# Two passes over 256 tokens in place of one over 512, in the gate and up products of four feed-forwards

## What is computed

```python
D_FF = ((8 * D_MODEL // 3 + 127) // 128) * 128      # 2816 = 22 * 128

def swiglu_2(h, w_gu, w_down):
    gu = h @ w_gu
    g, u = jnp.split(gu, 2, axis=-1)
    return (jax.nn.silu(g) * u) @ w_down

# twice (once for each layer):
h = modulate(x, g_norm[l, 0], mod[:, 0], mod[:, 1])
x = x + 0.5 * mod[:, 2][:, None, :] * swiglu_2(h, w_ffn1_gu[l], w_ffn1_down[l])
x = x + mod[:, 5][:, None, :] * hybrid_mixer(...)
h = modulate(x, g_norm[l, 2], mod[:, 6], mod[:, 7])
x = x + 0.5 * mod[:, 8][:, None, :] * swiglu_2(h, w_ffn2_gu[l], w_ffn2_down[l])
```

## Time and profile before

| | us |
|---|---|
| median of 2 runs (3003.88 and 3004.03) | 3003.95 |
| span of the profiled execution | 2999.2 |
| median less the span | 4.75 |
| PE busy (13,800 matmuls) | 2885.2 |
| PEld busy (13,800 weight loads) | 2294.2 |
| DVE busy | 1808.9 |
| ACT busy | 1307.9 |

### The profile page before, as it was taken

How to read it: one execution, slowest core, us unless ns; L and a number is a source line. 1 busy time by engine, 2 the same in 40 slices (tenths; PEclk the granted TensorE clock), 3 DMA queues, 4 the chain that set the end, 5 groups by cost and what they waited for, 6 DMA issues and landing times. The chain is left out here.

```text
span 2999.2 us, 39355 instructions
## 1 busy us (share of the span) xinstructions
PE 2885.2 (96%) x13800; PEld 2294.2 (76%) x13800; DVE 1808.9 (60%) x2177; ACT 1307.9 (44%) x1512; POOL 326.0 (11%) x425
## 2 busy tenths in 40 slices
PE   8999798999999999999999999999999999999998
PEld 4876566777777778888877788887888877788886
DVE  7747857999999987555158555425554156533323
ACT  5125535888888863233136322213322136332312
POOL 0100012333333320000000000000000000000000
PEclk9989999999999999999999999999999999999999
DMA  8552236999999996553222255423554222122221
GB/s 320 169 197 92 100 152 247 370 361 372 373 365 355 367 367 237 192 188 134 98 102 71 94 200 195 154 95 106 193 194 154 98 96 77 65 104 98 97 87 68
DMA packets 115843, 555.50 MB, mean 185 GB/s; under 512 B 20656, under 2 KB 22192, under 8 KB 73776
## 3 DMA queue, kind: packets, MB, share of 16 engines
q1 hardware_dynamic: 89264, 491.43, 44.3%
q0 software_dynamic: 26496, 62.96, 5.9%
HBM read 549.10 MB, written 37.75 MB: 196 GB/s over the span
## 5 line engine op out<-in xcount | busy, mean ns | idle before, releaser
L168 ACT ACTIVATE stream_high<-stream_raw 128x2048 fp32r<-128x2048 f32 x151 | 289.3, 1917 | 799.8 <-PE ffn_ps_psum L470 755.0
L173 DVE TENSOR_TENSOR stream_low<-stream_raw,stream_high 128x2048 fp32r<-128x2048 f32 x156 | 356.7, 2287 | 406.9 <-ACT stream_high L168 406.5
L468 PE MATMUL ffn_ps_psum<-h_high_f,stream_high 128*128 128x512 f32 x1344 | 523.3, 389 | 0.2 <-DVE stream_low L173 0.2
L470 PE MATMUL ffn_ps_psum<-h_high_f,stream_low 128*128 128x512 f32 x1344 | 522.8, 389 | 0.0
L469 PE MATMUL ffn_ps_psum<-h_low_f,stream_high 128*128 128x512 f32 x1344 | 522.8, 389 | 0.0
L312 DVE TENSOR_TENSOR expert_low<-expert_raw,expert_high 128x2048 fp32r<-128x2048 f32 x128 | 292.8, 2288 | 6.1 <-ACT expert_high L308 2.5
L692 DVE TENSOR_TENSOR ffn_sg<-ffn_sg,ffn_ps_psum 128x512 f32<-128x512 f32 x88 | 60.5, 687 | 388.5 <-PE ffn_ps_psum L470 385.6
L468 PEld LDWEIGHTS ffn_ps_psum<-h_high_f,stream_high 128*128 128x128 f32 x1344 | 252.3, 188 | 53.5 <-DVE stream_low L173 0.6
L469 PEld LDWEIGHTS ffn_ps_psum<-h_low_f,stream_high 128*128 128x128 f32 x1344 | 252.3, 188 | 52.8 <-issue 0.2
L470 PEld LDWEIGHTS ffn_ps_psum<-h_high_f,stream_low 128*128 128x128 f32 x1344 | 252.3, 188 | 51.8
L468 PE MATMUL ffn_ps_psum<-ffn_hid_high,stream_high 128*128 (+1 forms) x704 | 277.6, 394 | 3.2 <-DVE ffn_sg L692 3.2
(11 more groups left out here) (497 smaller groups left out, 5050.7 us busy)
## 6 DMA issues: line engine op xcount, KB each, us to landing
expert_raw<-in_exp_gu SPq DMA_DIRECT2D x128, 1024.0 KB
stream_raw<-in_ffn_gu SPq DMA_DIRECT2D x88, 1024.0 KB, 5.0
expert_raw<-in_exp_dn SPq DMA_DIRECT2D x64, 1024.0 KB
con<-in_w_mod SPq DMA_DIRECT2D x120, 512.0 KB
stream_raw<-in_ffn_dn SPq DMA_DIRECT2D x44, 1024.0 KB, 5.0
mix_mod_rows<-in_w_ada POOLq DMA_DIRECT2D x32, 512.0 KB
stream_raw<-in_w_in SPq DMA_DIRECT2D x16, 1024.0 KB, 5.0
pieces_raw<-in_w_in SPq DMA_DIRECT2D x11, 1024.0 KB, 6.9
```

The costliest lines, as they stand in the source:

```text
L168: self.nc.scalar.activation(self.high[:, q], self.raw[:, q], ACT.Copy).then_inc(self.high_done, 1)
L173: self.nc.vector.tensor_tensor(self.low[:, q], self.raw[:, q], self.high[:, q].bitcast(F32), ALU.subtract)\
L468: mm(out, w[0], x[0], start=start, stop=False)
L470: return mm(out, w[1], x[0], start=False, stop=stop)
```

## The change

Each of the three matmuls of a slice is made as two, over tokens 0 to 255 and 256 to 511, both with the same weights, into the two halves of the same bank. The `start` flag stands only on the first matmul of the bank, the `stop` flag only on the last. The semaphore increments stay on the last matmul of each bank.

```diff
+HALF_S = S // 2
...
                     def up_piece(s, bank, k):
                         c = slice((2 * k + bank) * P, (2 * k + bank + 1) * P)
-                        return self.mm3(ps[:, 2 * s + bank, :], w.part(s, c), (h[0][:, k, :], h[1][:, k, :]),
-                                        start=k == 0, stop=k == KD - 1)
+                        high, low = w.part(s, c)
+                        for weight, x in ((high, h[0]), (high, h[1]), (low, h[0])):
+                            for n in range(2):
+                                mm = nc.tensor.matmul(ps[:, 2 * s + bank, n * HALF_S:(n + 1) * HALF_S], weight,
+                                                      x[:, k, n * HALF_S:(n + 1) * HALF_S],
+                                                      start=k == 0 and x is h[0] and weight is high and n == 0,
+                                                      stop=k == KD - 1 and weight is low and n == 1)
+                        return mm
```

## The result

| | us |
|---|---|
| before, median of 2 runs | 3003.95 |
| after, median of 2 runs (3057.35 and 3064.43) | 3060.89 |
| ratio, with its 95% interval | 1.0193 (1.0161 to 1.0225) |
| span of the profiled execution after | 3062.3 |

The changed kernel is slower by 1.9%. Five more runs of it, beside nine of the kernel before on another chip, gave 3062.85 against 3011.15 us, a ratio of 1.0178 (1.0157 to 1.0198).

The account below looks back on a forecast made before the run. The prediction took the matmul stream's rate on PE as the bound. 4032 x (230.0 - 226.7) = +13.3 us on 3003.95 us gave 3017.3 us, with a range of 2990 to 3100 us.

Parts of the forecast that it names:

- What bounds the kernel: In the feed-forwards' up blocks only the matmul stream's rate sets the time; 4032 matmuls at 226.7 ns, 914 us.
- The counts and what hides: In the up blocks 4032 matmuls become 8064, with 4032 added weight loads; DVE, ACT and softer edges cost nothing.
- The weight load's rate: In the up blocks a load is hidden if the matmul beside it lasts 112 ns; fp32 rows gave 111.8 ns.
- Rival (D): Weight loads in the up blocks don't overlap: 188 ns for each matmul, 3606 us; chance 0.04.
- The loop's code: The up loop's body grows from 192 to 384 loads and matmuls; bound 20 us, nothing taken.
- Rival (C): The longer up loop doesn't stay on the chip, every round waits for code: up to +117 us, 3121 us; chance 0.07.
- The 13.3 ns: Each up matmul's time beyond its columns, taken as partly a rate: t = 115.0 ns for 256 columns, +13.3 us.
- rival (A): The extra is paid once for each up matmul: 120.0 ns for 256 columns, +53.6 us, 3057.6 us; chance 0.28.
- 0.43: Chance of the forecast's own case for the up matmuls, 2991 to 3030 us.
- 0.28: Chance that each up matmul pays the extra once, 3057.6 us.

Follow-up runs that it names:

- Experiments 3: Changed kernel with only the gate products split, the up products back in one pass of 512 tokens: 3033.58 us, ratio 1.0090 to the kernel before.
- 10: Changed kernel with the down products split in two halves of tokens as well: 3083.99 us, ratio 1.0251 to the kernel before.
- 4: Changed kernel with four passes of 128 tokens instead of two of 256: 3890.03 us in one run, kernel before 3011.15.
- 5: Changed kernel with each pass cut in 384 and 128 tokens instead of 256 and 256: 3247.68 us in one run, kernel before 3007.44.
- experiment 2: Changed kernel with all three products of one token half first, then those of the other: 3060.52 us, ratio 1.0167 to the kernel before.
- Experiment 6: Changed kernel with each slice multiplied for one half of the tokens only, 4032 matmuls of 256 columns: 2661.16 us in one run.
- experiment 9: Changed kernel, six of eight slices using 32 of 128 weight columns, 256 tokens in gate and 128 in up: 3035.99 us, kernel before 3007.22.
- experiments 7: Gate and up products with bf16 operands, in whole passes of 512 columns like the kernel before: 2974.90 us in one run, kernel before 3007.44.
- 8: Gate and up products with bf16 operands, in two passes of 256 columns like the changed kernel: 2976.56 us in one run, kernel before 3007.44.
- 12: Kernel before with feed-forward corrections in bf16, activations densely copied, products grouped by type, no split: 2979.09 us, ratio 0.9894 to the kernel before.

## Why the prediction came out as it did

**What bounds the kernel: right.** The stretches stayed full on PE at clock 1.00, and every nanosecond of spacing arrived in the time: 4032 x 13.3 ns = 53.6 us by the sum, and the same by the four stretches. Experiments 3 and 10 follow that sum with other counts, and 4 and 5 with the load's 111.7 ns where a matmul is shorter than its neighbour's load.

**The counts and what hides: right.** There are 8064 matmuls and as many loads; equal weights are loaded twice and don't matter (experiment 2); DVE, ACT and the softer edges cost nothing. Experiment 6 shows where that cover ends: when a block falls from about 10.9 to 5.8 us, DVE's splitting is late.

**The weight load's rate: right, as a floor.** 111.8 ns came from fp32 rows and was measured at 111.7 in fp32r (experiment 4). Rival (D), 188 ns, is out: the load's 192 ns are a latency and hide behind matmuls 120 ns apart. The page "TensorE: Matmul & The Clock Gate" of the Trainium skill, section "What overlaps and what doesn't", says that a load overlaps a running matmul only when it goes to other rows of the array; 8064 full 128 by 128 loads at 120.0 ns disagree with it.

**The loop's code: right to take nothing.** Rival (C) is out by the two instruction queues above and by experiment 4, whose body is four times that of before.

**The 13.3 ns: here the prediction failed.** The step is "I take the first, because a stretch that lies inside the duration looks like a rate": a 5 ns stretch for half the columns, t = 115.0. Measured were 120.0, with the duration at 283 ns against my 277. The term was 13.3 us and should have been 53.6, so the likeliest point lies 44 us below the measured median, and rival (A)'s 3057.6 us lies 3.3 below it. The range held because (A) was in it, and not by the forecast's own sum. That the kernels differ by less than 2% held narrowly: the ratio of 1.0178 lies below with its whole interval, that of 1.0193 reaches over it with the upper end of its own. That the part lies inside the duration told nothing of how it grows with columns; one 512-column size can't tell a rate from a start, and the trace had only that size in this type. So the choice between 0.43 and 0.28 rested on a likeness alone.

**The other half of that step was misleading too.** "It isn't the weight load", I wrote, since matmuls with 24-column weights are also 230 ns apart. For 256 columns the load does matter: 120.0 ns with 128 columns of weights, 113.3 with 32 (experiment 9). So rival (A) had the right time and not the right mechanism; a price of 13.3 ns whatever is loaded is refuted. It doesn't look like a rate either: with 32-column loads the extra is 6.7 ns for 256 tokens and 6.7 for 128.

**What stays open** is why fp32r pays this. Start to start less columns / 2.4, by size of tokens and weights: 512 and 128, 13.3 ns; 256 and 128, 13.3; 256 and 32, 6.7; 128 and 32, 6.7; 512 and 24, about 17 in the stretch of the earlier trace rows, where DVE was busy for 97% of the time. Two readings are left, both only argued.

The first: the moving operand comes in a little slower than the array takes it (6.7 ns for 256 columns, 13.3 for 512), a full load costs 13.3 ns of its own, and the larger of the two shows. It fits the first three values. The fourth should be 3.3; the short load's own rate could be what shows there, but the rows of 223 ns are shorter than those of 276 by just the 53 ns of 128 columns, so they show no wait for a load.

The second: the extra goes with the weight columns of the load and not with the tokens, 13.3 ns beside 128 and 6.7 beside 32. It fits the first four. Against it, none of the 14 spacings of the 24-column matmuls from 172.2 to 175.4 us is under 224 ns, 10.7 above the columns. And in fp32 a full load of 4-byte weights costs nothing like it, as the kernel before shows:

```profile
1107.81 4.45 PE L2737 MATMUL experts_x_psum<-hT,shared_wg 128*128 128x512 f32 x10
```

Ten starts, with a row of 592 ns for the last, are (4.45 - 0.59) / 9 = 429 ns each. At two steps a column 512 columns take 426.7 ns, so the extra is some 2.5 ns. So neither 4-byte operands nor their full loads bring the 13.3 ns by themselves. The size that would settle it, 512 tokens with 32 weight columns in a feed-forward stretch, wasn't run. What is shown: the extra belongs to fp32r operands (10.8 ns of it are gone in experiments 7 and 8), it is smaller with a short load (experiment 9), and with full loads each additional matmul of 256 columns costs 13.3 ns (the changed kernel, experiments 2, 3, 6 and 10).

**The 9.5 us ahead of the feed-forwards** are no part of any step; the change doesn't reach there, and runs of one kernel differ by as much.

## What to carry to other kernels

Read a dense stream's rate from its starts, take away columns / clock, and ask of the remainder how it depends on each operand; if the trace has only one size, the two readings are even until another size is measured. In fp32r with a full load for each matmul, two matmuls of 256 columns cost 13.3 ns more than one of 512, and below the load's own 112 ns fewer columns save nothing; in bf16 the split costs 2.5 ns. Of a product in three parts, the corrections can go in bf16; here that paid when they were densely laid and grouped by type, and not with neither (the two weren't tried apart).

## What the runs showed of the hardware

- fp32r, full 128 by 128 loads, start to start: 226.7 ns for 512 columns, 120.0 for 256, 111.7 for 128. With 32-column loads 113.3 for 256 and 60.0 for 128.
- bf16, full loads (98 ns long): 215.8 ns for 512 columns, 109.2 for 256. The 256-column bf16 stream ran below the 111.7 ns that is the floor of full fp32r loads, so with bf16 weights the floor is lower.
- A 384-column and a 128-column fp32r matmul in turn took 286.6 ns: the wide one's load, which starts beside the narrow matmul, isn't hidden.
- fp32, full loads, 512 columns: 429 ns, some 2.5 above two steps a column.
- bf16 read with a step of two as the moving operand: rows of 390 to 400 ns against 379, and 240 ns between two starts, in a stream that changes type twice in three matmuls. As the stationary operand the step cost nothing (experiments 7 and 12, 216 ns).
- Alternating one fp32r matmul with two bf16 ones took 700 ns a triple, more than three fp32r ones (680); in groups of 16 and 32 a block of 48 took 10.59 us, against 10.88 in fp32r and 10.53 by the sum of the two spacings.
